# The gate projections of a pool mixer, computed as seven block products for every two units

## The reference

```python
def pool_mixer(h, w_in, w_grp, scale, w_out):      # h is the normalised stream
    v, gate = split(h @ w_in)                      # each 2048 wide, 4 groups of 512
    u[g] = trailing mean of v[g] over (2, 4, 8, 16)[g] positions - v[g]
    u = (u @ w_grp) * scale
    return (u * silu(gate)) @ w_out
```

## Time and profile before

| | |
|---|---|
| time, median of 3 runs | 1564.74 us (1564.35 to 1564.80) |
| span of the profiled execution | 1563.4 us |
| what lies around the span | its own time is not listed apart; the median of the runs is 1.34 us above the span |
| PE busy | 1551.3 us, 99% of the span |
| DVE busy | 995.7 us, 64% |
| ACT busy | 604.3 us, 39% |
| stage A ends at about | 340.5 us of the span |

### The profile page before, as it was taken

How to read it: one execution, slowest core, us unless ns; L and a number is a source line. 1 busy time by engine, 2 the same in 40 slices (tenths; PEclk the granted TensorE clock), 3 DMA queues, 4 the chain that set the end, 5 groups by cost and what they waited for, 6 DMA issues and landing times.

```text
span 1563.4 us, 31492 instructions
## 1 busy us (share of the span) xinstructions
PE 1551.3 (99%) x13079; PEld 1393.3 (89%) x13079; DVE 995.7 (64%) x1590; ACT 604.3 (39%) x1102; POOL 353.4 (23%) x333
## 2 busy tenths in 40 slices
PE   9999999999999999999999999999999999999998
PEld 9999999999989898899898898888888988888887
DVE  6665565774866578576776667567615785676346
ACT  5323132253354343434444445573112246551121
POOL 0000000020421123031331214334430043343510
PEclk9999999999999999999999999999999999999999
DMA  5323223223221322221222133222233332222331
GB/s 169 109 81 103 87 82 92 98 81 114 64 75 55 88 78 83 82 83 55 83 83 95 56 112 103 82 81 81 83 107 135 108 102 82 82 81 81 109 134 54
DMA packets 113725, 141.14 MB, mean 90 GB/s; under 512 B 3020, under 2 KB 90480, under 8 KB 113584
## 3 DMA queue, kind: packets, MB, share of 16 engines
q1 hardware_dynamic: 109872, 134.38, 27.0%
q10 hardware_dynamic: 3632, 4.53, 1.0%
q0 software_dynamic: 80, 0.20, 0.0%
HBM read 137.01 MB, written 2.10 MB: 89 GB/s over the span
## 4 chain that ended last, share of the span: by engine, by line
PE 99%; DVE 1%; issue 0%; ACT 0%; POOL 0%; ACTq 0%; POOLq 0%
PE acc L398 28%; PE acc L400 28%; PE acc L399 28%; PE aux L544 2%; PE aux L398 1%; PE aux L400 1%; PE aux L399 1%; PE aux L609 1%; PE aux L611 1%; PE aux L1329 1%; PE aux L1359 1%; PE aux L601 1%; PE aux L1348 1%; PE aux L1349 0%; PE aux L1383 0%; PE aux L621 0%
## 5 line engine op out<-in xcount | busy, mean ns | idle before, releaser
L398 PE MATMUL acc<-xhis,whi 128*128 128x264 f32 (+2 forms) x1848 | 611.9, 331 | 0.0
L400 PE MATMUL acc<-xhis,wlo 128*128 128x264 f32 (+2 forms) x1848 | 602.3, 326 | 0.0
L399 PE MATMUL acc<-xlos,whi 128*128 128x264 f32 (+2 forms) x1848 | 601.8, 326 | 0.0
L400 PEld LDWEIGHTS acc<-xhis,wlo 128*128 128x128 f32 x1848 | 347.9, 188 | 29.4
L398 PEld LDWEIGHTS acc<-xhis,whi 128*128 128x128 f32 x1848 | 348.0, 188 | 29.0 <-issue 0.8
L399 PEld LDWEIGHTS acc<-xlos,whi 128*128 128x128 f32 x1848 | 348.3, 188 | 26.6
L393 POOL TENSOR_TENSOR wlo<-raw,whi 128x1024 fp32r<-128x1024 f32 x84 | 207.8, 2475 | 376.9 <-DVE whi L2460 376.9
L389 ACT ACTIVATE whi<-raw 128x1024 fp32r<-128x1024 f32 x158 | 164.3, 1049 | 131.5 <-PE acc L400 119.4
L393 DVE TENSOR_TENSOR wlo<-raw,whi 128x1024 fp32r<-128x1024 f32 x81 | 99.8, 1236 | 36.9 <-ACT whi L389 36.8
L2157 DVE TENSOR_TENSOR wlo<-raw,whi 128x1024 fp32r<-128x1024 f32 x77 | 93.8, 1221 | 22.4 <-ACT whi L389 22.3
L2460 DVE CAST whi<-raw 128x1024 fp32r<-128x1024 f32 x84 | 66.7, 796 | 54.0 <-PE acc L400 53.8
(11 more groups left out here) (378 smaller groups left out, 2800.8 us busy)
## 6 DMA issues: line engine op xcount, KB each, us to landing
raw<-in_w_in SPq DMA_DIRECT2D x38, 1024.0 KB, 5.3
raw<-in_hgrn_w_in SPq DMA_DIRECT2D x32, 1024.0 KB, 5.7
raw<-in_pool_w_in SPq DMA_DIRECT2D x15, 1024.0 KB, 5.4
raw<-in_pool_w_out SPq DMA_DIRECT2D x8, 1024.0 KB, 5.0
raw<-in_hgrn_w_out SPq DMA_DIRECT2D x8, 1024.0 KB, 5.5
raw<-in_w_out SPq DMA_DIRECT2D x8, 1024.0 KB, 5.0
raw<-in_pool_w_grp SPq DMA_DIRECT2D x4, 1024.0 KB, 5.2
raw<-in_w_branch_attn SPq DMA_DIRECT2D x4, 1024.0 KB, 4.9
```

The lines of the kernel that those rows point to most:

```text
L398: pe.matmul(dst, stat[0], mov[0], start=first, stop=False)
L399: pe.matmul(dst, stat[0], mov[1], start=False, stop=False)
L400: return pe.matmul(dst, stat[1], mov[0], start=False, stop=last)
```

## The change

In groups 1, 2 and 3 the four gate units become two pairs. A pair takes the 1024x256 weights of two units as four blocks (W11, W12 above, W21, W22 below, each 4 k tiles by 128), the stream as four blocks (k tiles 0 to 3 and 4 to 7, first and second 264 columns), and forms the 256x528 result from seven block products of 4 x 3 = 12 matmuls in place of eight. Around this it needs:

- **Sums of the stream**, four for each of four k (`sums`, on DVE, in the gate units of group 0), after the weighted stream has been multiplied by rstd into `xw`. ACT makes their hi parts (`sum_hi`, 1056 elements each), DVE the lo parts (`sum_lo`; the last as four of 264).
- **The normalised stream.** In group 0's `grp` units 0 and 1, `xhi` and `xlo` are made anew from `xw` (`xw_hi` and `xw_lo`, four of 528 elements on each of ACT and DVE in each of the two units). Groups 1 to 3 then need no rstd; their `v` accumulators are read out by ACT instead of DVE.
- **Sums of the weights** (`w_sums`, three subtractions of 512 elements on DVE, and `w_last`, a fourth), in place in the raw buffer or in `t_sums`. A pair uses four pieces of the ring, of 1024, 1024, 1024 and 512 elements, where two units used two of 1024.
- **Sums of the products.** The first product is copied out by ACT (`m_one`), DVE makes `m_two` and `m_four`, three blocks of the result are adds on DVE (264 elements, one operand in PSUM), one is a copy on ACT. The fifth, sixth and seventh product go on top of what stands in banks 0, 2 and 3, so that the sixth waits for `m_four` and the seventh for the first of the three adds.
- `plan_a` and `ring_a` write the longer ring out; SP loads the same chunks in the same order. The products and `pe.sem_inc` on PE keep the counts of `acc_done`.

The core of the diff:

```diff
+PAIRED = ((1, "gate"), (2, "gate"), (3, "gate"))
...
+        def w_sums(dve, t):
...
+            dve.wait_ge(raw_landed[chunk % RAW], 16 * (chunk // RAW + 1))
...
+            dve.tensor_tensor(t3, w22, w12, ALU.subtract).then_inc(t_step, 1)
+            dve.wait_ge(t_step, 4 * pair + 1)
+            dve.tensor_tensor(w12, w12, w11, ALU.subtract).then_inc(t_step, 1)
+            dve.wait_ge(t_step, 4 * pair + 2)
+            dve.tensor_tensor(t2, w22, w12, ALU.subtract).then_inc(t_step, 1)
...
+        def ring_lo(dve, t):
+            if A_RING[t + 1:t + 2] and A_RING[t + 1][0] == "pair" and A_RING[t + 1][2] == 0:
+                w_sums(dve, t + 1)
+            dve.wait_ge(hi_ready, PA + t + 1)
+            dve.tensor_tensor(ring_piece(wlo, t), ring_view(t), ring_piece(whi, t), ALU.subtract).then_inc(lo_ready, 1)
+            if A_RING[t][0] == "pair" and A_RING[t][2] == 2:
+                w_last(dve, t)
...
+            def pair_unit(pair, u, r):
...
+                if after:
+                    drained(pair - 1)
+                pe.wait_ge(acc_done[0], UA // 2 + u // 2)
+                product(b0, r, 0, of_block(0, 0), True).then_inc(prod_done, 1)
+                if after:
+                    drained_last(pair - 1)
+                pe.wait_ge(acc_done[1], UA // 2 + u // 2)
+                product(b2, r, 1, of_sum(1), True).then_inc(prod_done, 1)
+                product(b1, r + 1, 0, of_sum(2), True).then_inc(prod_done, 1)
+                product(b3, r + 1, 1, of_sum(3), True).then_inc(prod_done, 1)
+                pe.wait_ge(m_copied, 2 * pair + 1)
+                product(b0, r + 2, 0, of_block(0, 4), False).then_inc(prod_done, 1)
+                pe.wait_ge(m_step, 5 * pair + 2)
+                product(b2, r + 2, 1, of_sum(4), False).then_inc(lin_done, 1)
+                pe.wait_ge(m_step, 5 * pair + 3)
+                product(b3, r + 3, 0, of_block(1, 4), False).then_inc(lin_done, 1)
...
+            def sums(k):
...
+                for n, part in ((k, lo), (k + 4, up)):
+                    dve.scalar_tensor_tensor(out=part, in0=h[:, n, :], scalar=vec1[:, NW0 + n:NW0 + n + 1],
+                                             in1=rstd[:, :], op0=ALU.mult, op1=ALU.mult).then_inc(sum_step, 1)
...
+                dve.wait_ge(sum_step, 6 * k + 2)
+                dve.tensor_tensor(s1, x21, x22, ALU.add).then_inc(sum_step, 1)
+                dve.tensor_tensor(s3, x11, x21, ALU.subtract).then_inc(sum_step, 1)
+                dve.wait_ge(sum_step, 6 * k + 3)
+                dve.tensor_tensor(s2, s1, x11, ALU.subtract).then_inc(sum_step, 1)
+                dve.wait_ge(sum_step, 6 * k + 5)
+                dve.tensor_tensor(s4, x12, s2, ALU.subtract).then_inc(sum_step, 1)
...
+            def pair_vector(pair, G, n, u, r):
...
+                dve.tensor_tensor(m_two, b1, m_one, ALU.add).then_inc(m_step, 1)
...
+                dve.tensor_tensor(m_four, b2, m_two, ALU.add).then_inc(m_step, 1)
+                ring_lo(dve, r + 3)
...
+                dve.tensor_tensor(ga[:, n + 1, TH:T], b3, m_four, ALU.add).then_inc(m_step, 1)
+                ring_lo(dve, r + 4)
+                if n == 0:
+                    u_lo(G, 3)
+                ring_lo(dve, r + 5)
+                dve.wait_ge(lin_done, UA + u + 1)
+                dve.tensor_tensor(ga[:, n + 1, 0:TH], b2, m_two, ALU.add).then_inc(m_step, 1)
+                if n:
+                    for x in range(2):
+                        silu_a(G, n - 2 + x)
+                dve.wait_ge(lin_done, UA + u + 2)
+                dve.tensor_tensor(ga[:, n, TH:T], b3, m_two, ALU.add).then_inc(m_step, 1)
+                ring_lo(dve, r + 6)
...
+                if G == 0 and stage == "gate":
+                    if n:
+                        sum_lo(n - 1)
+                    sums(n)
+                if G == 0 and stage == "grp" and n < 2:
+                    if n == 0:
+                        sum_lo(3)
+                    for x, k in enumerate(((0, 4, 1, 5), (2, 6, 3, 7))[n]):
+                        xw_lo(4 * n + x, k)
```

More of the change, by code:

```diff
@@ L288, in program @@
         lnb = xns[:, :, :].rearrange("p s t -> p (s t)")[:, 0:D]
+        t_sums = sqs[:, :, :].rearrange("p s t -> p (s t)")[:, 0:1024].rearrange("p (k n) -> p k n", k=4)
+        m_flat = xns[:, :, :].rearrange("p s t -> p (s t)")
+        m_one, m_two, m_four = (m_flat[:, TH * n:TH * n + TH] for n in range(3))
+        s_sums = vpads[:, :, META:META + T].rearrange("p s (h t) -> p s h t", h=2)
         junk = sqs[:, :, :].rearrange("p s t -> p (s t)")[:, 0:D]
@@ new lines, in ring_hi @@
+        def ring_hi(act, t):
+            kind, chunk, q, pair = A_RING[t]
+            act.wait_ge(raw_landed[chunk % RAW], 16 * (chunk // RAW + 1))
+            if kind == "pair" and q != 2:
+                act.wait_ge(t_step, 4 * pair + (2, 3, None, 4)[q])
+            what, count = A_FREED[t - PIECES]
+            if what == "pair":
+                act.wait_ge(prod_done, count)
+            else:
+                act.wait_ge(lin_done, UA + count)
+            act.activation(ring_piece(whi, t), ring_view(t), ACT.Copy).then_inc(hi_ready, 1)
@@ L1166, in out_a_pair @@
                         mm.then_inc(lin_done, 1)
[L1169 to L1185, removed]
-                        rhs = lambda k, t0, w: (uhi[:, k, t0:t0 + w], ulo[:, k, t0:t0 + w])
-                        k_wait = (lambda k: pe.wait_ge(ulo_ready, 4 * G + k + 1)) if n == 0 else None
-                    elif stage == "out":
-                        rhs = lambda k, t0, w: (zhia[:, k, t0:t0 + w], zloa[:, k, t0:t0 + w])
-                        k_wait = None
-                    else:
-                        rhs, k_wait = of_x, None
-                    unit(pe, u % 2, kind, m, half, KT if kind == "k8" else GT, rhs, T, k_wait)
@@ new lines, in product @@
+            def product(bank, t, b, x_of, first):
+                whole = {} if first else {"skip_group_check": True}
+                hi, lo = piece(whi, "k4", t), piece(wlo, "k4", t)
+                cols = slice(P * b, P * b + P)
+                pe.wait_ge(lo_ready, PA + t + 1 + CREDIT)
+                for k in range(4):
+                    high, low = x_of(k)
+                    pe.matmul(bank, hi[:, k, cols], high, start=first and k == 0, stop=False, **whole)
+                    pe.matmul(bank, hi[:, k, cols], low, start=False, stop=False, **whole)
+                    mm = pe.matmul(bank, lo[:, k, cols], high, start=False, stop=k == 3, **whole)
+                return mm
```

494 lines of the change are left out of this document (340 added, 154 removed).

## The result

The changed kernel takes 1587.53 us (median of 4 runs, 1585.95 to 1588.21), the kernel before 1564.55 in the runs beside it: a ratio of 1.0146, 95% interval 1.0132 to 1.016, so 23 us slower.

What follows compares the result with a forecast made beforehand. TensorE was taken to bound the kernel, on 99% of the chain that ended last. -8.7 saved, +15.5 in group 0 and +11.2 in groups 1 to 3 give +18.0 us, say 1583; the range 1576 to 1590 holds 0.8.

Steps and rivals of the forecast that it cites:

- the forecast's own band: Whole kernel: all terms as sized within a fifth, 1576 to 1587 us, chance 0.70.
- the one for a dearer clock or dearer hand-overs: Whole kernel: clock or hand-overs cost more than priced, 1587 to 1592 us, chance 0.16.
- The saving: Six pairs in groups 1 to 3: 72 matmuls fewer at 0.1206 us each, 8.7 us off.
- The walk: Step through the engines' queues, by prices from the timelines, to find where TensorE waits: 15.5 and 11.2 us.
- The bound from the 0.56 row: VectorE's 264-element passes priced by the dearer row, 0.14 us more each: +23 us in all.
- the rival in which sums cost half: Passes reading SBUF alone run twice as fast: +4, 1568.5 us; chance 0.09 shared with group 0 hidden.
- Group 0: VectorE's added stream work makes TensorE wait in the group and out units: 15.5 us more.
- The clock: Group 0's group units: one or two run at half clock, adding at most about 1 us; not in the sum.
- The rival: TensorE's clock stays down into group 0's out units, 11.6 for 5.8 us; with dearer hand-overs 1587 to 1592, chance 0.16.
- Groups 1 to 3: Waits of TensorE in and behind the pairs: 3.2, 3.3 and 4.7 us, together 11.2.
- the twelve semaphore operations: `sem_inc` on TensorE, twelve times: between nothing and 0.1 us each, taken as nothing.
- The rival on the other side: Whole kernel: the vector work hides and only TensorE's 8.7 us come off, 1556 us, chance 0.04.

Runs made afterwards that it cites:

- e5_no_sums_at_all: Changed kernel without any stream or weight sums, constants in their buffers; seven products and hand-overs stay: 1563.49 us, ratio 0.9991 to the kernel before.
- e3_clock_kept_up: Changed kernel plus 61 TensorE matmuls on constants that fill its idle time in group 0's group and output units: 1584.44 us, ratio 1.0130.
- e1_no_stream_sums: Changed kernel without group 0's added work (scaled stream, its sums, their parts), constants in the sums' tiles; pairs and weight sums stay: 1570.55 us, ratio 1.0041.
- e4_high_sums_first: Changed kernel with ScalarE making the stream sums' high parts ahead of its wait for the unit in group 0's gate units: 1582.85 us, ratio 1.0119.
- e10_first_pair_on_gpsimd: Changed kernel with e4_high_sums_first's order, two more moves on VectorE, and each group's first pair's four weight sums on GpSimd: 1578.26 us, ratio 1.0093.
- e6_weight_sums_on_gpsimd: Changed kernel with all four weight sums of each pair on GpSimd instead of VectorE, the fourth written over W11: 1590.47 us, ratio 1.0169.

## Why the prediction was nearly right

The direction, the place and the mechanism were as forecast; the time was 4.5 us above the 1583. That is inside the range of 1576 to 1590, but half a us beyond the 1587 that closes the forecast's own band, in the one for a dearer clock or dearer hand-overs, which had 0.16. The miss has three parts of the same sign: 1.5 us in group 0 (the clock), 1.6 in groups 1 to 3 (hand-overs above all) and 1.5 behind the stage, whose cause is open.

**The saving.** 72 matmuls, 8.7 us: the count is shown, and e5_no_sums_at_all shows the 8.7 in the stage's end, 3.6 us earlier beside some 5 of waits.

**The prices on VectorE.** The walk had no row of 264 elements and took 0.42 us for it, 0.34 to the next start. Measured in the changed kernel:

```profile
49.21 0.43 DVE L2235 TENSOR_TENSOR vpads<-xw 128x264 f32<-128x264 f32 x1
49.56 0.42 DVE L2236 TENSOR_TENSOR vpads<-xw 128x264 f32<-128x264 f32 x1
49.91 0.43 DVE L2238 TENSOR_TENSOR vpads<-vpads,xw 128x264 f32<-128x264 f32 x1
50.37 0.43 DVE L2240 TENSOR_TENSOR vpads<-xw,vpads 128x264 f32<-128x264 f32 x1
```

The starts are 0.35 apart, 0.46 where one waits for another, as forecast. The bound from the 0.56 row and the rival in which sums cost half are both out.

**Group 0.** The gate read-outs were put at 52.1, 59.8 and 67.5 and come at 52.14, 59.88 and 67.61. TensorE's group units and outputs were put at 60.7, 68.5, 76.9, 82.0 and 87.0:

```profile
60.63 0.39 PE L441 MATMUL acc<-uhi,whi 128*128 128x264 f32 x1
...
68.37 0.59 PE L441 MATMUL acc<-uhi,whi 128*128 128x264 f32 x1 [4.53 <-DVE ga L2332]
...
76.78 0.59 PE L441 MATMUL acc<-uhi,whi 128*128 128x264 f32 x1 [3.86 <-DVE pz L2344]
...
86.88 0.36 PE L441 MATMUL acc<-zhia,whi 128*128 128x264 f32 x1 [1.74 <-DVE wlo L555]
...
88.30 0.44 PE L441 MATMUL acc<-zhia,whi 128*128 128x264 f32 x1 [0.45 <-DVE zloa L2371]
```

So 15.5 of the 17.0 us were forecast, each place to within 0.15. The list of waits was less exact in two: the third is shorter in the profile (3.9 for 5.5), since the unit before it ran slowly and ended late, and the fourth isn't in it at all, for the same reason. A slow clock that hides behind another wait takes that wait's place in the list. The row at 86.88 names `wlo`, which was done at 86.09; what ended that wait is VectorE's third `pz`, done at 86.78, as forecast:

```profile
86.01 0.77 DVE L2344 SCALAR_TENSOR_TENSOR pz<-acc,vec,ga 128x528 f32<-128x528 f32 x1
```

**The clock.** This term was left out of the sum: the prediction said that one or two group units would be slow at the cost of at most about 1 us, since VectorE sets the end. The two slow stretches among the group units did cost nothing (e3_clock_kept_up). But in the output units, where TensorE no longer waits for VectorE, the clock was low too (0.54 from 88.3 to 92.0), and that cost 1.5 us. The six matmuls behind the wait of 1.7 us still started 0.12 apart; those 0.22 apart stand behind the next wait, of 0.45. The rival had the whole first pair of output units at half speed, 5.8 us more; the clock was low for the first part of it only.

**Groups 1 to 3.** Forecast 11.2 us of waits, measured 12.4 from the starts of the matmuls on either side. The fifth product in group 3 was put at 1.6 and waits 1.42 by the profile (1.70 from start to start), the seventh at 1.05, 1.6 and 1.6 (starts 1.02, 1.54 and 1.54 apart, where 0.12 is usual), the first group unit at 1.55, 0.9 and 0.9 (1.58, 1.18, 1.18). The term that was under-sized is the hand-over to TensorE where one of the twelve semaphore operations, which I had put at nothing, stands between the wait and the matmul: before the second product of the second pair (0.6 forecast, starts 0.91 to 0.94 apart) and before the first group unit. The first two rows below are such a hand-over, from an add's end at 149.00 to 149.33; the last two, before a seventh product, have no such operation between, from 145.43 to 145.49:

```profile
148.58 0.42 DVE L2279 TENSOR_TENSOR ga<-acc,xns 128x264 f32<-128x264 f32 x1
149.33 0.36 PE L1284 MATMUL acc<-shi,whi 128*128 128x264 f32 x1 [0.65 <-PEq L1302]
...
145.00 0.43 DVE L2268 TENSOR_TENSOR ga<-acc,xns 128x264 f32<-128x264 f32 x1
145.49 0.39 PE L1284 MATMUL acc<-xhis,whi 128*128 128x264 f32 x1 [0.73 <-DVE ga L2268]
```

In all six such places it is 0.29 to 0.33 us where 0.13 was allowed, about 1 us together. The successor that comes 0.20 behind a waiting matmul was in the forecast. No run took the operations out, so their part is read from the rows alone. e1_no_stream_sums, forecast at 1567 from 11.2 less 8.7 and measured at 1570.55, holds the same deficit (1.7 us more than forecast in groups 1 to 3) and 1.4 us behind the stage. One price was worked out wrongly, without effect: the line through ScalarE's rows gives 0.34 us for 264 elements, not 0.31, and ScalarE's rows show 0.27 to the next start (145.75 to 146.02).

**Behind the stage.** Forecast no change; 1.5 us more, waits "issue" of TensorE in the later stage, 4.5 us for 2.9. Over the thirteen profiles this stretch lasts 1222.1 to 1224.9 us, and runs with more of these waits are the longer ones. No run changed one thing in it, so its cause is open.

**The rival on the other side**, the saving alone, falls with its condition: VectorE's turn in a gate unit is 7.7 us, and even at 6.5 (e4_high_sums_first) TensorE waits. No version here is faster than the kernel before. The fastest that computes the whole scheme, e10_first_pair_on_gpsimd, gets 9 of the 23 us back.

## What to carry to other kernels

A scheme that trades a matmul for additions is paid by the engine that adds: before writing it, walk that engine's queue through the stage where it is fullest, by start-to-start times, and find the first read-out that TensorE wants from behind the new work. Bound the gain by a kernel in which the additions are left out; if that one isn't faster, as here, moving those additions about can't save it. And before moving such work to GpSimd, look at what VectorE does at that moment: two-input work in SBUF on both takes turns.

## What the runs showed of the hardware

- VectorE and GpSimd took turns by whole instructions when both read SBUF and VectorE had two inputs there: two passes that take 1.44 us together lasted 3.58, one of 0.71 lasted 1.68 to 1.79, and GpSimd's sums of 1.29 between them 1.61 to 1.64. An addition with an input in PSUM lasted 0.71 beside a busy GpSimd.
- After TensorE's idle time of 4.5 us the granted clock was 0.51 of full speed, 1.2 GHz, and again behind those of 3.9 us and of 1.7 and 0.45 us, with matmuls 0.22 us apart instead of 0.12; in e6_weight_sums_on_gpsimd it stayed at 1.00 behind the same 1.7 and 0.46. With the idle time filled by products that nothing reads it stayed at 1.00. This is what the Trainium skill, "TensorE: Matmul & The Clock Gate", "HAM oscillation — how this bites in real kernels", leads one to expect of the first stretch; what it cost, 1.5 us, depended on where VectorE set the end anyway, and that is only in the timeline.
- At the full clock a matmul behind one that waited started 0.19 to 0.23 us after it, where 0.12 is usual. With a semaphore operation of TensorE's own between wait and matmul, the matmul started 0.29 to 0.33 us after VectorE's end, without one 0.05 to 0.06 us in the three seventh products.
